# A two-layer hybrid decode step: prompt heads in three score banks, full value tiles, a short mask, and the second gelu moved into the first page sequence

## The reference

```python
q_nope, q_pe = rms_norm(...), rope(rms_norm(...))
# prompt: causal attention over 256 rows, 8 heads
s = (q_nope . k_nope + q_pe . k_pe) * ATTN_SCALE
p = softmax(where(mask, s, NEG_INF));  y_at = p @ v
# sample: the same over 16 pages of 128 cached rows per sequence, 8 sequences, and the 8 new rows
k_nope, v = expand_kv(lat, w_ukv)           # lat: cached latent, 256 wide
# spatial gating: third branch
v = layer_norm(gelu(v_raw));  s = tril(w_s) @ v + b_s;  y_cm = gelu(u) * s
# merge, output projection, SwiGLU
x = x + sum_n(sigmoid(g_n) * (y_n @ w_branch_n)) @ w_out
x = x + (silu(h @ w_gate) * (h @ w_up)) @ w_down
```

## Time and profile before

| | |
|---|---|
| device time, median of 3 runs | 1580.42 us (1580.07 to 1581.97) |
| the profiled execution's own time | 1581.96 us |
| its span (first to last instruction) | 1580.0 us |
| PE, DVE, ACT, POOL busy | 98%, 67%, 56%, 33% |
| DMA | 142 GB/s |

### The profile page before, as it was taken

The page is one execution under the profiler, slowest core; times in us unless marked ns, Lnnn a source line. Parts: engine busy times, 40 slices in busy tenths (PEclk is TensorE's granted clock), DMA queues, the critical chain, the costliest instruction groups (busy, mean ns, idle before and its releaser), DMA issues.

```text
span 1580.0 us, 33275 instructions
## 1 busy us (share of the span) xinstructions
PE 1550.8 (98%) x10796; PEld 1507.2 (95%) x10796; DVE 1056.6 (67%) x1620; ACT 891.5 (56%) x1740; POOL 524.7 (33%) x709
## 2 busy tenths in 40 slices
PE   7999999999999999999999999999999999999999
PEld 7987999999999999999998789999999999999999
DVE  6777767776664766664376877777775658666633
ACT  5787776777533444443357877677764335444432
POOL 3723377676600000000048224777766001000000
PEclk9999999999999999999999999999999999999999
DMA  7331454553645444444454224545436444444443
GB/s 277 121 102 51 117 171 145 147 149 104 187 132 156 148 146 149 152 153 146 146 189 130 77 66 118 179 141 153 139 117 178 138 157 147 147 146 148 155 148 113
DMA packets 114722, 224.65 MB, mean 142 GB/s; under 512 B 12881, under 2 KB 78706, under 8 KB 114482
## 3 DMA queue, kind: packets, MB, share of 16 engines
q1 hardware_dynamic: 112178, 214.75, 44.1%
q0 software_dynamic: 2432, 8.49, 1.6%
HBM read 220.73 MB, written 2.46 MB: 141 GB/s over the span
## 4 chain that ended last, share of the span: by engine, by line
PE 81%; DVE 5%; ACT 4%; issue 3%; POOL 2%; POOLq 2%; DVEq 2%; ACTq 1%; DMA 0%; SPq 0%
PE PS L820 53%; PE PS L1075 20%; DVE w_lo L1768 1%; PE PS L1105 1%; PE PS L1106 1%; POOL r_lo L751 1%; ACT w_hi L1321 1%; POOLq L724 1%; DVEq L1762 1%; ACT r_hi L1321 1%; PE PS L876 1%; ACT lt_hi L1321 1%; PE PS L847 1%; POOL q_rot L711 0%; DVEq L2049 0%
## 5 line engine op out<-in xcount | busy, mean ns | idle before, releaser
L1768 DVE TENSOR_TENSOR w_lo<-raw,w_hi 128x1024 fp32r<-128x1024 f32 x258 | 324.9, 1260 | 221.3 <-ACT w_hi L1321 218.4
L1321 ACT ACTIVATE w_hi<-raw 128x1024 fp32r<-128x1024 f32 x258 | 272.2, 1056 | 348.6 <-PE PS L820 334.4
L820 PE MATMUL PS<-h_hi,w_hi 128*128 128x320 f32 x1360 | 425.9, 313 | 11.2 <-DVE h_lo L1795 10.4
L820 PE MATMUL PS<-h_lo,w_hi 128*128 128x320 f32 x1360 | 420.8, 309 | 0.0
L820 PE MATMUL PS<-h_hi,w_lo 128*128 128x320 f32 x1360 | 420.7, 309 | 0.0
L820 PEld LDWEIGHTS PS<-h_hi,w_hi 128*128 128x128 f32 x1360 | 255.9, 188 | 14.6 <-issue 9.6
L820 PEld LDWEIGHTS PS<-h_lo,w_hi 128*128 128x128 f32 x1360 | 256.0, 188 | 1.0
L820 PEld LDWEIGHTS PS<-h_hi,w_lo 128*128 128x128 f32 x1360 | 255.9, 188 | 0.0
L1321 ACT ACTIVATE ksqp<-PS 128x512 f32<-128x512 f32 x256 | 152.6, 596 | 135.4 <-PE PS L1075 131.6
L2109 DVE TENSOR_REDUCE kss<-ksqp 128x8 f32<-128x512 f32 x256 | 173.2, 680 | 80.5 <-ACT ksqp L1321 79.8
L1075 PE MATMUL PS<-comb_hi,lt_hi 128*128 128x288 f32 x1024 | 224.0, 300 | 3.0 <-DVE lt_lo L1771 1.5
(11 more groups left out here) (325 smaller groups left out, 2683.8 us busy)
## 6 DMA issues: line engine op xcount, KB each, us to landing
raw<-in_stream SPq DMA_DIRECT2D x258, 512.0 KB, 3.5
tpage<-in_tcache SPq DMA_DIRECT2D x256, 160.0 KB, 2.3
rrow<-in_rcache SPq DMA_DIRECT2D x256, 128.0 KB, 2.7
x<-in_xT SPq DMA_DIRECT2D x2, 640.0 KB, 7.0
sbias<-in_sbias POOLq DMA_DIRECT2D x2, 640.0 KB, 6.5
out_yT<-x SPq DMA_DIRECT2D x4, 320.0 KB, 2.2
const<-in_consts SPq DMA_DIRECT2D x1, 1090.0 KB
wgate<-in_wgate POOLq DMA_DIRECT2D x2, 512.0 KB, 4.4
```

The source lines that it names most:

```text
L820: done = mm(out, w[:, slot, c], a, start=first and n == 0 and m == 0, stop=last and n == len(pairs) - 1 and m == 2)
L1321: return nc.scalar.activation(out, in_, func, **kw)
L1768: V.tensor_tensor(w_lo[:, s, :], raw[:, s, :], f(w_hi[:, s, :]), ALU.subtract).then_inc(lo_done.sem, 1)
```

## The change

- **Prompt heads.** Scores use banks 0, 1, 2 in turn and run three heads ahead; the 256-column part comes first and opens the bank, and the mask is one fp32r matmul of two diagonal blocks (256 columns) at the end. Probabilities are transposed in banks 3 and 5; `PAIR_BANK` is (4, 6, 7, 6). SCALE is folded into the query gains, so DVE's maxima come out negated and the multiplication and its drain go.
- **Value tiles.** `vp` becomes two tiles with 128 columns for every head, 64 of them zero (filled by POOL and DVE); both heads of a pair add into one bank over all partitions.
- **New scores** move from before head 0 to after the spatial transposes; their two masks (POOL) move into sequence 0, page pairs 3 and 4.
- **Second gelu.** The square moves to POOL, ahead of the pages. In sequence 0: DVE arguments in halves after pages 1 and 3; ACT loads the tanh table after page 3, does tanh in halves after 5 and 7, reloads the log/exp table after 9; splits after 1 and 11; rounds `y2_hi` in halves after 13 and 15. POOL multiplies gate and rows (`sgu_p`) at page pairs 1 and 2. DVE: gated products after 7 and 9, weight rests after 5 and 13, `y2_lo` after 15 and in sequence 1 after page 1. The buffer fills and `p_free` move later.
- **Queries.** POOL places the absorbed part at page pair 5 and the rotary part at 6, in every sequence.
- **DMA.** States, convolution rows and `vrows` go out by SP instead of POOL; the sample values' weights come by SP in sequence 1's order; SP no longer waits for `sgu_y`.
- **First round.** SP issues the weight units `u + 2`, `u + 3` and `u + 4` each one batch of rows later (row pairs 6 and 7 of sequence 6, then 0 and 1, then 2 and 3 of sequence 7, now come ahead of them); ACT rounds row pair 1 ahead of gate 5; DVE normalises and copies values ahead of a split.

```diff
-PAIR_BANK = (4, 6, 7, 5)
+PAIR_BANK = (4, 6, 7, 6)
+PROB_BANK = (3, 5)
...
             def scores(h):
-                b = h % 2
+                b = h % 3
                 pe.wait_ge(bank_free[b].sem, banks.take(l, b))
-                mm(PS[:, b, 0:384], ident_r[:], mask_r[:], start=True, stop=False)
-                for qt, c0, n in ((0, 0, 128), (1, 128, 256)):
+                for qt, c0, n in ((1, 128, 256), (0, 0, 128)):
...
+                diagonal = PS[:, b, 0:384].rearrange("p (n k) -> p n k", n=3)[:, 0::2]
+                mm(diagonal, ident_r[:], mask_r[:].rearrange("p (o k) -> p o k", o=1).to_broadcast([128, 2, 128]),
+                   start=False, stop=True).then_inc(ps_mm.sem, 1)
...
-                o = PS[64 * (h % 2):64 * (h % 2) + 64, ob, :]
-                mm(o[:, 0:256], vp[:, 0, 64 * h:64 * h + 64], pT[:, h % 2, 0:256], start=True, stop=False)
-                mm(o[:, 128:256], vp[:, 1, 64 * h:64 * h + 64], pT[:, h % 2, 256:384], start=False, stop=True).then_inc(ps_pv.sem, 1)
+                cols = slice(128 * h, 128 * h + 128)
+                mm(PS[:, ob, 0:256], vp[0][:, cols], pT[:, h % 2, 0:256], start=h % 2 == 0, stop=False)
+                mm(PS[:, ob, 128:256], vp[1][:, cols], pT[:, h % 2, 256:384], start=False, stop=h % 2 == 1).then_inc(ps_pv.sem, 1)
...
             for h in range(H):
-                if h + 2 < H:
-                    scores(h + 2)
-                b = 2 + h % 2
+                if h + 3 < H:
+                    scores(h + 3)
+                b = PROB_BANK[h % 2]
...
# ACT, sequence(l, b, par)
-                if not tail and p in (4, 8):
-                    split(l, U_D + p // 4 - 1)
-                if not tail and p == 10:
+                if not tail and p == 3:
+                    tanh_table()
+                if not tail and p in (5, 7):
+                    spatial_tanh(l, p // 2 - 2)
+                if not tail and p == 9:
                     log_and_exp_tables()
+                if not tail and p in (1, 11):
+                    split(l, U_D + p // 11)
+                if not tail and p in (13, 15):
+                    spatial_hi(l, p // 2 - 6)
...
# POOL, sequence(b, par)
+                    if c in (1, 2) and first:
+                        part = slice(2 * c - 2, 2 * c)
+                        nc.gpsimd.tensor_tensor(va[:, part], va[:, part], ua[:, part], ALU.mult).then_inc(sgu_p.sem, 1)
+                    if c == 3 and first:
+                        pool.drain()
+                        new_scores_masked()
+                        pool.drain()
+                    if c == 4 and first:
+                        other_sequences_masked()
+                        pool.drain()
...
-                    if c == 6 and not last:
+                    if c == 5 and not last:
...
-                        queries(b + 1, 1 - par)
+                        place_high(b + 1, 1 - par)
+                        pool.drain()
+                        place_low(b + 1, 1 - par)
+                    if c == 6 and not last:
+                        rope_high(b + 1, 1 - par)
+                        pool.drain()
+                        rope_low(b + 1, 1 - par)
+                        pool.drain()
+                        rope_mask(b + 1, 1 - par)
...
# DVE
+            for g in (0, 2):
+                V.tensor_tensor(va[:, g:g + 2, :], PS[:, 4 + g:6 + g, 0:T], sbias[:, g:g + 2, :], ALU.add)
+                release(4 + g)
+                release(5 + g)
...
-                V.tensor_reduce(cols[:, 0:1], PS[:, h % 2, 0:128], AX.X, ALU.max)
-                V.tensor_reduce(cols[:, 1:2], PS[:, h % 2, 128:384], AX.X, ALU.max)
-                dve.drain()
-                V.tensor_scalar_mul(cols[:, 2:4], cols[:, 0:2], -SCALE).then_inc(ps_max.sem, 1)
+                V.tensor_reduce(cols[:, 0:1], PS[:, h % 3, 0:128], AX.X, ALU.max, negate=True)
+                V.tensor_reduce(cols[:, 1:2], PS[:, h % 3, 128:384], AX.X, ALU.max, negate=True).then_inc(ps_max.sem, 1)
...
# SP, end of the pages
             weights(l, u + 1)
-            weights(l, u + 2)
             load_rows(l, q, 6, of)
             load_rows(l, q, 7, of)
-            weights(l, u + 3)
+            weights(l, u + 2)
...
# ACT, first round
-            for j in (4, 5):
-                gate(l, 0, j)
-                split(l, U_D + j + 3)
-                page_rows_hi(l, b, j - 4)
+            gate(l, 0, 4)
+            split(l, U_D + 7)
+            page_rows_hi(l, b, 0)
+            page_rows_hi(l, b, 1)
+            gate(l, 0, 5)
+            split(l, U_D + 8)
...
# DVE, first round
+            copy_values(l, b)
             split(l, U_D + 12)
-            copy_values(l, b)
```

More of the change, by code:

```diff
@@ L35 @@
 EPS = 1e-6
-LOG_EXP_SET = 6
+LOG_EXP_SET, TANH_SET = 6, 0
 SCALE = float((DN + DR) ** -0.5)
@@ L767, in sequence @@
                         nc.gpsimd.memset(mx[HT:128], 0.0)
-                        pool.drain().then_inc(p_free.sem, 1)
+                        pool.drain()
+                    if c == 2 and second:
+                        pool.wait_ge(y2_ready.sem, y2_ready.at(l, 1))
+                        pool.sem_inc(p_free.sem, 1)
                     if values and c == 0:
@@ L968, in spatial_and_attention_inputs @@
             last.then_inc(latT_mm.sem, 1)
-            pe.wait_ge(kT_ready.sem, kT_ready.at(l, 1))
-            pe.wait_ge(bank_free[3].sem, banks.take(l, 3))
-            pe.wait_ge(qpz_ready.sem, qpz_ready.at(l, 3))
-            mm(PS[0:TS, 3, :], kpe[:, SEQ:T], qpz[:, :, SEQ:T], start=True, stop=False)
-            for j in range(4):
-                last = mm(PS[0:TS, 3, 128 * j:128 * j + 128], kT[:, j, SEQ:T], qz[:, 2 * j:2 * j + 2, SEQ:T],
-                          start=False, stop=j == 3)
-            last.then_inc(sn_mm.sem, 1)
         def v_transposed(l, c, b):
@@ L1022, in prompt_attention @@
             v_transposed(l, 2, 7)
+            pe.wait_ge(bank_free[3].sem, banks.take(l, 3))
+            mm(PS[0:TS, 3, :], kpe[:, SEQ:T], qpz[:, :, SEQ:T], start=True, stop=False)
+            for j in range(4):
+                last = mm(PS[0:TS, 3, 128 * j:128 * j + 128], kT[:, j, SEQ:T], qz[:, 2 * j:2 * j + 2, SEQ:T],
+                          start=False, stop=j == 3)
+            last.then_inc(sn_mm.sem, 1)
             pe.wait_ge(vp_ready.sem, vp_ready.at(l, 2))
+            scores(2)
             for h in range(H):
-                if h + 2 < H:
-                    scores(h + 2)
-                b = 2 + h % 2
+                if h + 3 < H:
+                    scores(h + 3)
+                b = PROB_BANK[h % 2]
                 pe.wait_ge(ps_prob.sem, ps_prob.at(l, h + 1))
@@ L1612, in seq_exp, with tanh_table, spatial_tanh, spatial_hi @@
                 act.wait_ge(p_split.sem, p_split.at(l, b * 4))
-            A(prob[:], nope(par), ACT.Exp, scale=SCALE)
-            A(snp_hl[:, 0:HT], snp[:], ACT.Exp, scale=SCALE)
-            A(snp[:], snp[:], ACT.Exp, scale=SCALE).then_inc(s_exp.sem, 1)
+            A(prob[:], nope(par), ACT.Exp)
+            A(snp_hl[:, 0:HT], snp[:], ACT.Exp)
+            A(snp[:], snp[:], ACT.Exp).then_inc(s_exp.sem, 1)
+        def tanh_table():
+            act.add_instruction(mybir.InstLoadActFuncSet(name=nc.get_next_instruction_name(), act_func_set_id=TANH_SET,
+                                                         engine=mybir.EngineType.Activation, ins=[], outs=[]))
+        def spatial_tanh(l, g):
+            act.wait_ge(garg.sem, garg.at(l, 2 + g))
+            part = slice(2 * g, 2 * g + 2)
+            A(ge[:, part], ge[:, part], ACT.Tanh, scale=GELU_C).then_inc(gth.sem, 1)
+        def spatial_hi(l, g):
+            act.wait_ge(sgu_y.sem, sgu_y.at(l, g + 1))
+            part = slice(2 * g, 2 * g + 2)
+            A(y2_hi[:, part], ge[:, part], ACT.Copy, scale=0.5).then_inc(y2h.sem, 1)
         def sequence(l, b, par, tail=True, last=False):
@@ L2110, in sequence @@
                 if not tail and p in (1, 3):
-                    part = slice(p - 1, p + 1)
-                    dve.wait_ge(y2h.sem, y2h.at(l, 1))
-                    done = lo(y2_lo[:, part], ge[:, part], y2_hi[:, part])
-                    if p == 3:
-                        done.then_inc(y2_ready.sem, 1)
-                if not tail and p in (5, 9):
-                    split(l, U_D + p // 4 - 1)
-                if not tail and p == 7:
+                    spatial_argument(l, p // 2)
+                if not tail and p in (7, 9):
+                    spatial_gated(l, p // 2 - 3)
+                if not tail and p in (5, 13):
+                    split(l, U_D + p // 13)
+                if not tail and p == 15:
+                    spatial_lo(l, 0)
+                if isinstance(b, int) and b == 1 and p == 1:
+                    spatial_lo(l, 1).then_inc(y2_ready.sem, 1)
+                if isinstance(b, int) and b == 1 and p == 3:
                     dve.wait_ge(sn_ready.sem, sn_ready.at(l, 1))
```

239 lines of the change are left out of this document (125 added, 114 removed).

## The result

The changed kernel takes 1583.06 us (median of 22 runs, 1581.48 to 1584.54) against 1580.62 us for the one before (22 runs): ratio 1.0014, 95% interval 1.0008 to 1.002. The difference lies within the 0.2% that counts here as no change; the interval leaves out 1, so it is a small loss. Forecast were 1569.2 us and a range of 1562 to 1578. The likeliest case, 11 us faster, did not come. The kernel before and three of the experiments' kernels each had one far slower execution (1866 to 3752 us); it is in their medians, which it moves by 0.4 us at most, and in no comparison of stages.

What follows compares the result with a forecast made beforehand. PE, busy 98% of the span, bounds the kernel, so only matmul time and PE's waits count. 2 x 3.8 (prompt) + 6.8 (queries, first round) - 2 x 1.6 (sequence 0) = 11.2 us, giving 1569.2 us; range 1562 to 1578.

Steps and rivals of the forecast that it cites:

- The bank wait: Prompt attention: the first value product's 1.08 us wait for bank 4, freed by DVE, goes; 1.1 us gained per layer.
- the issue waits at the value products: Prompt heads: weight loads idle 0.17 us at each change of tile width; full 128-column tiles save 0.34 us a head.
- the first rival: Prompt heads bound by the DVE and ACT chain, or 0.17 us not tile width: 1.9 us per layer, 1573 us; chance 0.12.
- I get about 1 us left: 0.3 gained: End of prompt heads: the 1.23 us wait for the last probabilities shrinks to about 1 us, gaining 0.3 per layer.
- The tanh load after page 3 is short by 0.7 us: Sequence 0: ACT's tanh table load before `pages_hi` exceeds the slack, costing PE 0.7 of 1.6 us lost per layer.
- The places after pages 9 and 11: Sequence 0: ACT's table reload after page 9 and split after page 11 each fall short by 0.4 us.
- VectorE's own items after odd pages are free: Sequence 0: DVE's added items follow odd pages, where it has no `lt_lo`, so they cost nothing.
- ends five waits and one for `q_rot` per layer: Queries placed at pair 5: `q_rot` and `r_lo` come about 0.8 us earlier, ending these PE waits.
- POOL in DVE's way: Rival, sequence 0: POOL's products block DVE's `lt_lo`, losing 4.6 us per layer, 1578.4 us; chance 0.10.
- The rival that the queries' new place costs more: No POOL room at page pair 5: everything behind comes 1.3 us later in five sequences per layer, 1585.6 us; chance 0.06.
- the 6.8 us: Queries and first round together: ended PE waits with their refilling, 6.8 us gained over both layers, bounds 4 and 8.
- Half of the prompt gain: Rival: prompt stage gives only 1.9 us per layer, 1573 us, about 1576 with sequence 0 at its bad bound; chance 0.12.

Runs made afterwards that it cites:

- the filler: Changed kernel plus a memset of a 128x32 scratch tile and a drain on GpSimd ahead of `r_lo` of page pair 3: 1575.21 us.
- The kernel that reached 1568.54 us: Changed kernel with ScalarE's sequence 0 items one page earlier, second split after page 14, `pair_lo(l, 0)` after last normalising, memset before pair 3's `r_lo`: 1568.54 us, ratio 0.992.

## Why the prediction was wrong

- *Prompt heads.* The bank wait and the issue waits at the value products in the heads went, and a head in which no step waits takes 2.42 us, as forecast (a whole one does in the run with the first pair's low part later): values 0.66 for 0.79, transposes 0.32 for 0.42. But not every head is such a one. The head shown takes 2.53, and the one ahead of it 2.87, with a wait for `pT`; in layer 1 that head takes 3.24. This is the mechanism of the first rival, a chain through ScalarE, which the sum gave nothing; it makes 0.37 of the 0.59 us by which layer 1 gained less than layer 0. (The prediction's head of 2.80 us was also the shortest of the steady ones before: its neighbours took 2.93 and 3.04.) The larger step that failed is "I get about 1 us left: 0.3 gained" for the tail. It rested on durations laid in the new order by hand, and missed that `pair_lo(0)` needs `y_hi`, which ScalarE can give only after its own earlier items, with head 6 queued behind. It cost 1.4 us a layer; with it moved, the stages came to 27.2 and 27.6 us against the 27 forecast, and the gains to 3.5 and 2.9 us against 3.8.
- *Sequence 0.* "The tanh load after page 3 is short by 0.7 us" was right to 0.04 us. The places after pages 9 and 11 cost 0.39 together (0.26 at page 12, 0.13 at page 14) and not 0.8; VectorE's split after page 5, which the sum had at nothing, cost 0.46, for `w_lo` ran 2.02 us beside GpSimd's product. With ScalarE's items a page earlier it ran 1.22 us and page 8 lost nothing. The step that failed is that VectorE's own items after odd pages are free: the second `w_lo` stands ahead of `lt_lo` of sequence 1 and cost 0.74. Measured +2.3 a layer, forecast +1.6, and avoidable down to 0.06. (By the prediction's own terms, 0.9 + 0.86 + 0.7 against 3.16 us, the slack was 0.7 and not 0.6; that changes little.)
- *Table loads.* The load in the new place ends at 142.26 + 1.28 = 143.54, and the next activation starts at 143.55, as in the earlier trace rows. The 1380 ns that the Trainium skill adds for a drain ("ScalarE: Activation LUTs", What ACT_TABLE_LOAD costs) do not show here either; the measurement decides.
- *Queries.* The waits ended, and PE was 0.44 us ahead at page 1 of sequence 4 and 0.46 at page 5, which is the size forecast, but 0.21 at page 7. The step that failed is the sum: "ends five waits and one for `q_rot` per layer" was booked as time won, without asking where GpSimd and VectorE stand once everything behind comes 0.4 us earlier. At page 8 some 0.6 us were lost, in each of eight stages (and 0.1 at page 9). The rival *POOL in DVE's way* had the right mechanism, mostly at the wrong place: I looked for it in sequence 0, where GpSimd got new work and it struck once (page 8), and not in the steady sequences, where its work had only been moved. The trace of the kernel before had the very meeting, in sequence 2, and its row of four waits for `lt_lo` would have led there. The rule of the Trainium skill ("SBUF — State Buffer", Who interferes with whom) that the ports the two engines share are locked and the order of issue decides who blocks is what the runs show: 1.70 and 1.19 us in one order, 0.68 and 1.54 in the other.
- *The rival that the queries' new place costs more.* Its mechanism, no room at pair 5, isn't what happened: the filler adds work and wins.
- *First round.* Forecast as part of the 6.8 us; the stage gave 3.16, `olat` and the long row wait gone as forecast.
- *Sequence 1.* "Nothing" was 0.36 us a layer. By starts 0.3 of it is lost at page 8, by the meeting of `kp_lo` and VectorE's product at page 7. In the traces of all fifteen kernels the two go together: 2.34 us from page 7 to page 8 where the product takes 0.90 to 0.98 us, 2.04 in the kernel before, where `kp_lo` takes the longer time, and 2.12 in the four stages, all in layer 1, where `kp_lo` comes 0.45 us later. No run was made to order this one on purpose.
- *Half of the prompt gain*, at its worst, was put at about 1576 us; 3.8 + 6.8 - 7.8 gives 1577.6. The range holds either.

The kernel that reached 1568.54 us does by three changes of order and a memset what the sum had promised. That the totals agree (12.1 us for 11.2) is in part luck: sequence 0 came out 3.1 us better than the sum had it, the prompt 1.1 and sequence 1 0.8 worse, and 1.5 us are the old meeting in sequence 2, which was never in the sum.

## What to carry to other kernels

A wait ended is not time won until the next place where two engines can meet has been laid out with the new starts: lay the two queues side by side for a whole steady stage, and look for starts within some tenths of a microsecond of each other, and in the trace of before for meetings that are there already. Where the meeting is decided by 0.04 us, order it on purpose, and so that the engine with slack pays; a small delay of that engine did better here than a semaphore, which delayed it by 0.8 us more and so made the next meeting. In an in-order queue, put an item that waits for a late producer behind those that are ready.

## What the runs showed of the hardware

A 128x512 `lt_lo` on VectorE took 0.68 us when it started ahead of GpSimd's `r_lo` and 1.70 when it started 0.04 us behind it; `r_lo` took 1.19 when first and 1.54 when 0.2 us behind. The second one ended 0.55 and 1.06 us after the end of the first, 0.13 less than it takes alone: it was held for all of the first but that. A shift of 0.25 us between two engines' starts was worth 0.6 to 0.8 us in each stage of sequences 2 to 6, and 7.8 us in the kernel.
